# Hybrid decoder layer on one core: the forgetting attention's transposes moved between the two halves of a dense unit, and a copy at the start moved up

## The reference, cut to what matters

```python
h   = rmsnorm(x, g_mix)
p   = h @ w_in                         # q, k, v of two attentions, and forget logits
yA  = dilated_attention(...)           # three head groups, mixed by their softmax denominators
yB  = forgetting_attention(qb, kb, vb, cum_logf)   # 8 heads, causal, softmax(q k + c_q - c_k) v
gates = sigmoid(h @ w_gate + b_gate)
x1  = x + (gates[:d] * (yA @ w_proj_a) + gates[d:] * (yB @ w_proj_b)) @ w_out
x2  = x1 + shared_swiglu(rmsnorm(x1)) + top-8-of-64 experts' swiglu(rmsnorm(x1))
```

## Time and profile before

| what | value |
|---|---|
| median of 3 runs | 1102.56 us (1102.43 to 1103.54) |
| the profiled execution's own time | 1102.48 us |
| its span | 1100.7 us |
| PE busy | 1081.0 us, 98% of the span |
| DVE busy | 882.3 us, 80% |
| ACT busy | 739.3 us, 67% |
| granted TensorE clock, mean | 0.997 of full speed |

### The profile page before, as it was taken

The page is one execution under the profiler, slowest core; times in us unless marked ns, Lnnn a source line. Parts: engine busy times, 40 slices in busy tenths (PEclk is TensorE's granted clock), DMA queues, the critical chain, the costliest instruction groups (busy, mean ns, idle before and its releaser), DMA issues.

```text
span 1100.7 us, 19484 instructions
## 1 busy us (share of the span) xinstructions
PE 1081.0 (98%) x5823; PEld 892.3 (81%) x5823; DVE 882.3 (80%) x1405; ACT 739.3 (67%) x1304; POOL 299.2 (27%) x288
## 2 busy tenths in 40 slices
PE   8999999999999999999999999999999999999995
PEld 7789988877777887678888888888888888888884
DVE  6543386478865835589999999999999999999993
ACT  6434465544346521268888888888888888888883
POOL 1221021000000001125433333344434444434442
PEclk9999999999999999999999999999999999999998
DMA  7243212421522093679999999999999999999982
GB/s 250 78 116 109 83 51 66 153 77 40 138 112 97 11 380 142 251 257 371 387 391 386 375 388 381 380 371 388 383 382 384 389 381 383 382 373 386 366 271 37
DMA packets 97353, 284.71 MB, mean 259 GB/s; under 512 B 19683, under 2 KB 22251, under 8 KB 96924
## 3 DMA queue, kind: packets, MB, share of 16 engines
q1 hardware_dynamic: 78876, 250.52, 59.6%
q0 software_dynamic: 18432, 33.61, 12.5%
HBM read 279.79 MB, written 37.81 MB: 289 GB/s over the span
## 4 chain that ended last, share of the span: by engine, by line
PE 91%; DVE 5%; ACT 1%; DMA 1%; issue 1%; POOL 1%; SPq 0%; ACTq 0%; POOLq 0%
PE bank L1849 32%; PE bank L1670 23%; PE bank L1863 17%; PE bank L1877 5%; PE bank L1823 3%; PE bank L1612 3%; PE bank L1837 3%; PE bank L1857 1%; DVE w_lo L1092 1%; PE bank L1697 1%; PE bank L1726 1%; PE bank L1739 1%; PE bank L1936 1%; PE bank L1715 1%; DMA arena<-in_x 0%
## 5 line engine op out<-in xcount | busy, mean ns | idle before, releaser
L1849 PE MATMUL bank<-gu_parts,xT_parts 128*128 128x512 f32 x1280 | 338.7, 394 | 0.0
L1849 PEld LDWEIGHTS bank<-gu_parts,xT_parts 128*128 128x128 f32 x1280 | 235.4, 188 | 45.9
L1863 PE MATMUL bank<-w_lo 128*128 128x512 f32 x804 | 201.6, 399 | 0.0
L1863 PEld LDWEIGHTS bank<-w_lo 128*128 128x128 f32 x804 | 146.3, 188 | 28.5 <-issue 0.5
L605 POOL TENSOR_TENSOR turn<-minus_half 16x1 f32<-16x1 f32 x123 | 73.6, 599 | 335.0 <-DMA out<-arena,idxs 174.4
L616 POOL DMA_INDIRECT out<-arena,idxs x64 | 124.7, 1948 | 46.0 <-issue 15.0
L1670 PE MATMUL bank<-w_hi,hT_hi 128*128 128x512 f32 (+1 forms) x320 | 124.8, 390 | 1.4 <-DVE arena L1187 0.7
L1670 PE MATMUL bank<-w_hi,hT_lo 128*128 128x512 f32 (+1 forms) x320 | 121.8, 381 | 0.0
L1670 PE MATMUL bank<-w_lo,hT_hi 128*128 128x512 f32 (+1 forms) x320 | 121.6, 380 | 0.0
L1452 DVE TENSOR_TENSOR gu_parts<-arena,gu_parts 128x1024 fp32r<-128x1024 f32 x96 | 116.6, 1215 | 0.4 <-PE bank L1837 0.3
L1452 DVE TENSOR_TENSOR gu_parts<-arena_x,gu_parts 128x1024 fp32r<-128x1024 f32 x96 | 116.6, 1215 | 0.1
(11 more groups left out here) (228 smaller groups left out, 1903.9 us busy)
## 6 DMA issues: line engine op xcount, KB each, us to landing
arena<-in_w_gate_e SPq DMA_DIRECT2D x64, 512.0 KB
arena<-in_w_up_e SPq DMA_DIRECT2D x64, 512.0 KB
arena<-in_w_down_e SPq DMA_DIRECT2D x64, 512.0 KB
arena_x<-in_w_gate_e SPq DMA_DIRECT2D x64, 512.0 KB
arena_x<-in_w_up_e SPq DMA_DIRECT2D x64, 512.0 KB
arena_x<-in_w_down_e SPq DMA_DIRECT2D x64, 512.0 KB
arena<-in_w_in SPq DMA_DIRECT2D x14, 1024.0 KB, 5.6
arena<-in_w_gate SPq DMA_DIRECT2D x8, 1024.0 KB, 5.6
```

The source lines that it names most:

```text
L1849: last = nc.tensor.matmul(out_, a[:, PER * c + j, :], b[c][:, :, j, :], start=(c == 0 and j == 0 and i == 0), stop=(c == CHUNKS - 1 and j ...
L1863: last = nc.tensor.matmul(psY[h][0:rows, :], midT[n][a][:, j, 0:rows], w[b][:, j, h * 512:(h + 1) * 512], start=(j == 0 and k == 0), stop= ...
```

## The change

PE's order in each of the 16 steps becomes: scores, the first 12 matmuls of the gate unit, the wait for the weights, their transposes, the other 12 matmuls, the statistics, the weighted sum. `dense` gets an argument for the blocks it does. No matmul, transpose or copy is added or removed, and the orders of DVE and ACT in these steps stay as they are.

At the start DVE copies the first half of tile 0 of the turned x before it makes the mean of tile 1, not after it; the second half stays behind the mean. The wait for the constants goes with the first half.

```diff
             norm_x(0)
+            dve.wait_ge(const_in, 32)
+            copy_wide(("x", 0), hT, gmixT, (0,))
             dve.wait_ge(squared, 2)
             means[0] += 1
             nc.vector.tensor_scalar(hn_ms[:, 1:2], hn_ss[:, 1:2], 1.0 / D, EPS, ALU.mult, ALU.add).then_inc(mean_ready, 1)
-            dve.wait_ge(const_in, 32)
-            copy_wide(("x", 0), hT, gmixT)
+            copy_wide(("x", 0), hT, gmixT, (1,))
             dve.wait_ge(rnorm_ready, means[0])
...
-            def dense(n):
-                for j in range(ND):
+            def dense(n, blocks=range(ND)):
+                for j in blocks:
                     dense_step(n, j)
...
                 if v < UB:
                     scores_b(v)
+                dense(B_UNITS + v - 1, range(HALF))
                 pe.wait_ge(weights_scaled, v)
                 for s in range(2):
                     c0 = s * width_b(v - 1)
                     transposes(("pb", v - 1, s), [(sc_b[(v - 1) % 2][:, c0 + b * P:c0 + (b + 1) * P], P) for b in range(tile_b(v - 1) + 1)])
-                dense(B_UNITS + v - 1)
+                dense(B_UNITS + v - 1, range(HALF, ND))
```

## The result

The changed kernel takes 1106.75 us (median of 8 runs, 1105.43 to 1109.68) against 1103.49 us before (8 runs, 1102.43 to 1104.07): a ratio of 1.0035, 95% interval 1.0025 to 1.0044. It is slower, by 3.3 us between the medians and by 3.9 us (2.8 to 4.9) by the ratio. The direction was forecast, with 1105.3 us and a chance of 0.60; the size was forecast at 2.85 us. The profiled execution of after happens to be the longest of its eight: 1109.68 us, span 1107.9.

The account below looks back on a forecast made before the run. PE, busy 98% of the span, bounds the kernel. From 1102.48 us, -0.6 + 1.3 - 2.5 + 2.1 + 1.75 + 0.8 = +2.85 gives 1105.3 us, range 1102.9 to 1106.9.

Parts of the forecast that it names:

- The rival in which no wait takes the old one's place: DVE's copies of steps 6 and 10 end before PE needs them: 1101.5 us, or 1100.7 without the late gate; chance 0.13.
- The rival with held transfers: DVE's delay also makes the broadcast of the mixing weights land late in step 8: +1 us, 1106.3 us; chance 0.08.
- Change of operand kind: PE's dense unit starts twice per step, behind masks and behind transposes: 16 x 0.083 = +1.3 us, bounds 0 and 1.3.
- Weighted sum of step 6: PE there waits for DVE's copy of the turned weights, ending at 272.88 against PE's arrival at 270.8: +2.1 us.
- Step 10: PE's weighted sum there waits for DVE's copy, ending at 305.84 against PE's arrival at 304.1: +1.75 us.
- Late gate: In step 16 ACT's gate comes late and the projection waits for its bank: +0.8 us, bounds 0.5 and 0.9.
- The prediction's own two ends: Step 16, counted from the start of the transposes: ACT's chain ends 4.35 us behind it, the unit 0.6 + 2.8.
- Waits that go: PE's waits ahead of the transposes and for the bank in step 6, covered by 12 matmuls: -2.5 us.
- Part 1, the start: Half of tile 0's copy fits DVE's idle time before the mean of tile 1: -0.6 us, bounds 0 and 0.65.
- My rival in which the copy at the start gains nothing because a load ends the wait: A load holds the start, so the split copy wins nothing: 1105.9 us, counted inside the main case of 0.62.
- a term that was put at nothing: Granted clock read as 1.00 in all three stretches, upper level for waits and work; no cost for a fall.
- carried to the end one for one: From 350 us on PE runs almost without a gap, so its earlier gain or loss reaches the end in full.

Follow-up runs that it names:

- Experiment 3: Changed kernel with DVE's reciprocal and product moved to step 7 and its combinations to steps 10 and 11: 1101.96 us, ratio 0.9991 to the kernel before.
- experiment 4: The changed kernel unedited, run a second time for the spread between executions: 1105.11 us, ratio 1.0031 to the kernel before.
- experiment 7: Changed kernel with the new order in steps 12 to 16 only, its start kept: 1104.21 us, ratio 1.001 to the kernel before.
- experiment 2: Changed kernel with the loop's order put back, so the split copy at the start alone: 1103.08 us against 1102.87 before, ratio 1.0004.
- experiment 1: Changed kernel with the copy at the start put back, so the loop's new order alone: 1105.98 us, ratio 1.0029 to the kernel before.
- experiment 9: The changed kernel unedited, run a third time: 1106.47 us, ratio 1.0032 to the kernel before.
- experiment 8: Changed kernel with useless small matmuls on PE, 24 in step 6 and 16 in step 10, where it waits: 1106.04 us, ratio 1.0029 to the kernel before.

## Why the prediction was right in kind and off in size

**Right: the mechanism.** The waits of the transposes are gone. DVE's copy of step 6 ends at 272.84 in after, against 272.88 in the prediction, with the loop begun 0.3 us later than before. The weighted sums of steps 6 and 10 wait for DVE's copy, and the projection for ACT's gate. Experiment 3 shows that the two long waits need DVE's mixing work in those steps: the same order on PE without it has neither. The rival in which no wait takes the old one's place is refuted by these waits. The Trainium skill (Perfetto Trace Analysis, Optimization Strategy) advises to find the gaps of the bounding engine and what ends them; by PE's gaps alone that rival would have come out. The rival with held transfers is not seen: from 222 to 358 us no engine of after waits for a DMA.

**The terms of the loop**, from the profile without the fall (experiment 4), against the prediction:

- Change of operand kind: 1.3 forecast; experiment 7 gives 0.08 per step, and experiment 4 has the second start with 0.31 us. Right. The Trainium skill (TensorE: Matmul & The Clock Gate, Back-to-back issue gap) gives the gap between warm matmuls by a formula of their columns alone; by that this term would be 0, and the 0.08 disagrees.
- Weighted sum of step 6: +2.1 forecast, 1.88 measured. Step 10: +1.75 forecast, 1.28 at the weighted sum and 0.4 at the scores ahead of it, where PE waits for the row maxima: 1.7 together.
- Late gate: +0.8 forecast, 0.6 measured. That is near the bound of 0.5. The prediction's own two ends, 4.35 and 0.6 + 2.8 us, lie 0.95 apart; how 0.8 comes of that it does not show.
- Waits that go: -2.5 forecast. 2.85 - 1.3 - 1.88 - 1.7 - 0.6 = -2.6, what the loop's time leaves for it.

So the loop without the fall is worth +2.85, where my terms for it add up to +3.45: each of the new waits is a little smaller than worked out. That +2.85 is also the forecast of the whole is luck.

**Wrong: Part 1, the start, "I take -0.6 us".** Measured alone it is +0.4 us (-0.4 to +1.4, from the ratio). The step that failed is the one with the landings: DVE's idle time of 1.52 us was taken as there to be filled, and the first weights as landed in time ("a landing up to 11 us would not take the gain away"). I had read the landings of one execution as fixed. In the profiles the first use of tile 1 of x starts from 6.5 to 8.0 us. When it is early, DVE has no idle time there to fill (experiment 2). In the other six profiles with the split copy ACT waits 0.40 to 0.97 us for the first weights and starts their split at 11.05 to 11.79, beyond the 11 us; in before it followed the high part at 10.99 without idling. My rival in which the copy at the start gains nothing because a load ends the wait had named this. The first dense matmul starts between 12.23 and 13.29 in the seven profiles with the split copy, at 12.80 on average, and between 12.80 and 13.19, on average 13.05, in the four without it. A gain of some 0.2 us may be there; it is lost in a spread of 1 us. The lower bound of my range for this part, 0, would have been nearer.

**Wrong: a term that was put at nothing.** I read the granted clock of 1.00 in the three stretches as the clock of the changed kernel too, and priced the waits of steps 6 and 10 as idle time alone. In the profiles of after and experiment 1 the clock falls behind the 1.9 us wait of step 6 and costs 1.6 us more; in those of experiments 4 and 9, behind the same wait, it does not, and not behind the 1.3 us of step 10 in any of the four. In experiment 8, with the wait filled in part, and experiment 3, without it, there is no fall.

**What the sum would have been.** The loop +2.85, the start near 0, and for the fall, in two profiles of four, some 0.8 on average: about +3.6 us. Measured is +3.3 by the medians, in experiments 4 and 9 +2.2 and +3.8, and by the three ratios 3.4 to 3.9. In my sum the gain of 0.6 us at the start that didn't come and the loop's terms, 0.6 us too high, had cancelled by luck, and it was short by the fall. How often the clock falls in the timed executions stays open. Their mean clock is on record to 0.001, where a fall takes away 1.72 of some 1105 us, 0.0016: the 27 executions of the change average 0.9958, the 71 of the kernel before beside the experiments 0.9963. That would be a fall in about a quarter of them (an estimate, if nothing else lowers the clock), but experiment 2, which has no such wait, averages 0.9960. Experiment 8 didn't settle it either, so that the fall makes up the whole rest is not shown.

**Probably not the change's:** the late scatters at the end, and PE's lost time there. The tail is 752.9 us in after and 752.2 in experiment 3, but 750.3 in experiments 1, 4 and 9, which have the change's loop as well. So the prediction's "carried to the end one for one" holds in three profiles of the change's loop and not in the fourth. What brings the late scatters on was not tried and stays open, and so does whether they come more often with the change.

## What to carry to other kernels

A wait of the bounding engine that is covered by moving its instruction behind other work can come back at the next reader, if the engine that consumes the result works in order and has no idle time: follow the moved instruction to its consumer, and that consumer's other work to its next deadline. Here it paid to move the late engine's side work instead (one reciprocal of 3.34 us among it), and the order on PE only in the one step that then still waited: 1.0035 became 0.9979. A gain at the start that hangs on when loads land is to be taken from several executions, not from one.

## What the hardware showed beyond that

A wait of 1.9 us in the midst of dense matmul work was followed, in two of four profiles, by the lower clock level (1.2 GHz) somewhere between 272 and 278 us: 1.6 us on top of the wait. A wait of 1.28 us was not, in the same four profiles. With 24 small bf16 matmuls (1.51 us) in the place of the longer wait the one profile taken shows no fall.

On DVE a reciprocal of a 4x512 tile takes 3.34 us, where the addition of the same shape in front of it takes 0.68: one small instruction by its data, and the longest on the way to the late copy.

The landing of the first loads varies by over 1 us between executions of kernels that issue them alike, and so does the tail, by 2.6 us, with the last scatters. Both are large beside what this change was about.
